# Three transformer blocks on one core: ends of the mixers, projections and feed-forwards issued as one stream of units

## What is computed

```python
def block1(h):                      # 528 tokens
    h = h + mixer_1(rmsnorm(h))     # 3 attention branches; below is how the mixer ends
        # merged = sum over 3 branches of sigmoid(g_b + bias) * (y_b @ w_br_b); then merged @ w_out
    z = rmsnorm(h) @ w_up           # 2 x 2816 columns
    gate, val = split(z)
    return h + (silu(conv3(gate) + b) * val) @ w_down
def block2(x):
    x = x + mixer_2(rmsnorm(x) @ w_in) @ w_out
    x = x + same_feed_forward_form(rmsnorm(x))
    return rmsnorm(x)
def block3(h, c):
    sh1, sc1, g1, sh2, sc2, g2 = split(silu(c) @ w_ada + b_ada)
    h = h + g1 * (mixer_3((rmsnorm(h) * (1 + sc1) + sh1) @ w_in) @ w_out)
    h = h + g2 * (square(relu((rmsnorm(h) * (1 + sc2) + sh2) @ w_ff1)) @ w_ff2)
    return rmsnorm(h)
# rmsnorm(a) = a * rsqrt(mean(a*a over the 1024 features) + 1e-6) * gain
```

## Time and profile before

| | us |
|---|---|
| median of 3 runs | 3058.05 |
| the profiled execution | 3077.81 |
| its span | 3075.5 |
| TensorE matmuls busy (mean granted clock 0.941) | 2847.3 (93%) |
| TensorE weight loads busy | 2335.3 (76%) |
| VectorE busy | 1517.5 (49%) |
| ScalarE busy | 1066.4 (35%) |
| GpSimd busy | 101.6 (3%) |
| DMA, mean | 78 GB/s |

### The profile page before, as it was taken

The page is one execution under the profiler, slowest core; times in us unless marked ns, Lnnn a source line. Parts: engine busy times, 40 slices in busy tenths (PEclk is TensorE's granted clock), DMA queues, the critical chain, the costliest instruction groups (busy, mean ns, idle before and its releaser), DMA issues. The chain is left out here.

```text
span 3075.5 us, 40714 instructions
## 1 busy us (share of the span) xinstructions
PE 2847.3 (93%) x16096; PEld 2335.3 (76%) x16096; DVE 1517.5 (49%) x2420; ACT 1066.4 (35%) x1882; POOL 101.6 (3%) x89
## 2 busy tenths in 40 slices
PE   7999999899999979979988999898899899899998
PEld 6778888889999857867745788675676568678786
DVE  3786643644444462164454666543663453433443
ACT  3365444432222341423333322233332332332222
POOL 0053210000000000000000000000000000000000
PEclk9999999999999997879878999999999999999999
DMA  3111111222222312210002455332121112222221
GB/s 122 61 49 53 51 63 56 70 74 91 89 89 88 119 56 79 68 34 2 1 1 103 165 190 186 108 103 69 62 76 55 35 62 96 76 82 95 83 95 69
DMA packets 70834, 240.13 MB, mean 78 GB/s; under 512 B 12084, under 2 KB 12981, under 8 KB 70302
## 3 DMA queue, kind: packets, MB, share of 16 engines
q1 hardware_dynamic: 63054, 210.19, 20.6%
q10 hardware_dynamic: 7632, 27.86, 2.6%
HBM read 235.37 MB, written 2.64 MB: 77 GB/s over the span
## 5 line engine op out<-in xcount | busy, mean ns | idle before, releaser
L473 PE MATMUL ps<-xh,wh 128*128 128x258 f32 (+1 forms) x2352 | 721.7, 348 | 59.6 <-DVE xl L640 37.2
L473 PE MATMUL ps<-xl,wh 128*128 128x258 f32 (+1 forms) x2352 | 707.7, 342 | 0.0
L473 PE MATMUL ps<-xh,wl 128*128 128x258 f32 (+1 forms) x2352 | 705.2, 341 | 0.0
L473 PEld LDWEIGHTS ps<-xh,wh 128*128 128x128 f32 x2352 | 409.0, 191 | 132.0 <-issue 62.8
L418 ACT ACTIVATE wh<-ring 128x1024 fp32r<-128x1024 f32 x224 | 238.0, 1063 | 776.1 <-PE ps L473 765.9
L473 PEld LDWEIGHTS ps<-xl,wh 128*128 128x128 f32 x2352 | 408.4, 191 | 55.6 <-issue 5.7
L473 PEld LDWEIGHTS ps<-xh,wl 128*128 128x128 f32 x2352 | 409.4, 191 | 50.9
L432 DVE TENSOR_TENSOR wl<-ring,wh 128x1024 fp32r<-128x1024 f32 x224 | 274.3, 1225 | 316.2 <-ACT wh L418 316.1
L447 DVE TENSOR_TENSOR wl<-ring,wh 128x1024 fp32r<-128x1024 f32 x150 | 187.2, 1248 | 434.5 <-ACT wh L441 434.1
L455 PE MATMUL ps<-xh,wh 128*128 128x512 f32 x728 | 324.3, 446 | 27.3 <-DVE wl L447 13.6
L455 PE MATMUL ps<-xl,wh 128*128 128x512 f32 x728 | 297.8, 409 | 0.0
(11 more groups left out here) (395 smaller groups left out, 3352.9 us busy)
## 6 DMA issues: line engine op xcount, KB each, us to landing
ring<-in_weights SPq DMA_DIRECT2D x374, 512.0 KB, 3.5
arena<-in_w_ada ACTq DMA_DIRECT2D x48, 512.0 KB, 4.9
arena<-in_cmp_w SPq DMA_DIRECT2D x2, 2048.0 KB
h<-in_x ACTq DMA_DIRECT2D x4, 528.0 KB, 6.4
arena<-strip_scratch SPq DMA_DIRECT2D x8, 264.0 KB, 3.8
out_features<-arena SPq DMA_DIRECT2D x8, 256.0 KB, 2.2
tail<-in_nsa_consts SPq DMA_DIRECT2D x1, 1320.0 KB, 6.1
con<-in_consts SPq DMA_DIRECT2D x1, 801.0 KB, 11.3
```

Source lines behind the costliest of these rows:

```text
L473: last = pe.matmul(out(e), w[:, k, :], x[:, k, o:o + m], start=(k == 0 and n == 0), stop=(k == chunks - 1 and n == 2))
```

## The change

The plain functions, their blocks and their hardware loops are gone. `Merged`, `add_product`, the feed-forwards, the last norm of the second block and the modulation become stages of the same `run` as the projections that follow (`mixing_end` and second block's projections; `mixing_end_2` and the whole third block). Four `run`s remain, at whose ends engines meet: the first block's attention; from `Merged` to the second block's projections; the second block's attention; and one from its output projection to the end.

- `Line` replaces `Tiles` and the loops over tiles: units with a number of chunks, a choice of PSUM banks, and waits on whoever drained a bank last (`claim`).
- `Inputs` replaces input chunk k as soon as the last unit of the stage before has read it (`chunk_used`, semaphore `left`) and its source is ready.
- For norms without shifts (first feed-forward, second block's projections, second feed-forward), `Inputs` takes only the gain, and 1/norm is multiplied into the matmul's result: in `Glu` by GpSimd, once into the gate ahead of the convolution and once into the silu output; in the second block's `Projected` by VectorE, which then writes the tile in place of ScalarE's copy.
- `Sums` adds the squares of tiles 0 to 6 up on GpSimd, and TensorE multiplies only two tiles by ones (that sum and tile 7) instead of eight.
- `SecondRoot` derives the third block's first norm from sums taken before the second block's last norm is applied; `Residual` applies that one later. `Normed` is the old normed input with shifts.
- Behind the gate of the first feed-forward, 512 columns are computed instead of 516: the value units and the down product, each a single matmul of 512 columns where there were two of 258.
- `Modulation` takes two sums every 1.75 units, over 42 units.
- `Convolved`, `Gated` and `Merged` keep their work and get done-semaphores for the stage that reads them.

The core of the diff (`Added` is `add_product`'s addition as a `Line`, `Squared` is `act_mul`, `Later` shifts a stage's times):

```diff
+class Line(Stage):
...
+    def __init__(self, core, n, at, cols, banks, inputs=None, chunks=NC):
+        self.core, self.n, self.at, self.cols, self.banks, self.inputs, self.chunks = core, n, at, cols, banks, inputs, chunks
+        self.first, self.d = core.taken, chunks / NC
...
+        self.left = core.take("input_used", chunks - 1)
+        core.chunk_used = [(self.left.sem, self.left.at(k + 1)) for k in range(chunks - 1)] + [(core.used, core.taken)] + core.chunk_used[chunks:]
...
+    def claim(self):
+        core, self.opened = self.core, []
+        for u in range(self.n):
+            held = [self.bank(u) + b for _, _, b in self.pattern(u)]
+            waits = []
+            for b in held:
+                if b in core.drained and core.drained[b] not in waits:
+                    waits.append(core.drained[b])
+            self.opened.append(waits)
+            for b in held:
+                core.drained[b] = self.drain(u)
...
-                yield self.at + u + k / NC
+            wh, wl = core.wh[:, s % 2], core.wl[:, s % 2]
+            for k in range(self.chunks):
+                yield self.at + (u * self.chunks + k) / NC
                 if k == 0:
-                    if self.free.at(u - 1) > 0:
-                        pe.wait_ge(self.free.sem, self.free.at(u - 1))
+                    for sem, value in self.opened[u]:
+                        pe.wait_ge(sem, value)
                     pe.wait_ge(core.split_done, s + 1)
-                if self.x and u == 0:
-                    self.x.ready(pe)(k)
-                last = core.chunk(pe, s, k, lambda e: self.place(u), self.T, k == 0, k == NC - 1)
-            last.then_inc(core.used, 1)
+                if u == 0 and self.inputs:
+                    pe.wait_ge(self.inputs.lo.sem, self.inputs.lo.at(k + 1))
+                for i, (w, x) in enumerate(((wh, core.xh), (wh, core.xl), (wl, core.xh))):
+                    for e, (o, m, _) in enumerate(self.pattern(u)):
+                        last = pe.matmul(self.place(u, e), w[:, k, :], x[:, k, o:o + m], start=(k == 0 and i == 0),
+                                         stop=(k == self.chunks - 1 and i == 2))
+                if k == self.chunks - 1:
...
+class Inputs(Stage):
...
+        self.hi, self.lo = core.take("input_hi", len(tiles)), core.take("input_lo", len(tiles))
+    def scalar(self, act):
+        for k, a in enumerate(self.tiles):
+            yield self.at + (k + 1) / NC + 0.02
+            if self.free[k]:
+                act.wait_ge(*self.free[k])
+            if self.ready:
+                self.ready(act, k)
+            act.activation(self.core.xh[:, k, 0:self.T], a, ACT.Copy, scale=self.gains[k] if self.gains else 1.0).then_inc(self.hi.sem, 1)
+    def vector(self, dve):
+        for k, a in enumerate(self.tiles):
+            yield self.at + (k + 1) / NC + 0.14
+            dve.wait_ge(self.hi.sem, self.hi.at(k + 1))
+            xh, xl = self.core.xh[:, k, 0:self.T].bitcast(F32), self.core.xl[:, k, 0:self.T]
+            if self.gains:
+                ins = dve.scalar_tensor_tensor(out=xl, in0=a, scalar=self.gains[k], in1=xh, op0=ALU.mult, op1=ALU.subtract)
+            else:
+                ins = dve.tensor_tensor(xl, a, xh, ALU.subtract)
+            ins.then_inc(self.lo.sem, 1)
...
+class Normed(Stage):
...
+                                     in1=self.core.xh[:, k, 0:SEQ].bitcast(F32), op0=ALU.add, op1=ALU.subtract).then_inc(self.lo.sem, 1)
+        for k in range(NC):
+            yield self.at + 0.28 * k
+            if k == 0:
+                dve.wait_ge(self.columns.sem, self.columns.at(1))
+                dve.wait_ge(self.root.sem, self.root.at(1))
+            if k >= 2:
+                part(k - 2)
+                dve.wait_ge(self.lo.sem, self.lo.at(k - 1))
...
+class Sums(Stage):
...
+    def scalar(self, act):
+        core = self.core
+        for k in range(NC):
+            yield self.at + (k + 1) * self.d + 0.25
+            self.ready(act, k)
+            if k >= 2:
+                act.wait_ge(self.added.sem, self.added.at(max(1, k - 2)))
+            act.activation(self.sq[:, k % 2], self.tiles[k], ACT.Square, scale=self.gains[k] if self.gains else 1.0).then_inc(
+                self.squared.sem, 1)
+        yield self.end() + 0.55
+        if self.first is None:
+            core.exp_ln(act)
+            act.wait_ge(self.summed.sem, self.summed.at(1))
+            r = self.r.rearrange("p (s n) -> p s n", s=len(halves(self.T)))
+            core.act.do(act, act.activation(r, self.total(), ACT.Ln, bias=core.c("eps6"), scale=1.0 / D))
+            act.activation(self.r, self.r, ACT.Exp, scale=-0.5).then_inc(self.root.sem, 1)
+    def pool(self, pool):
+        for k in range(1, NC - 1):
+            yield self.at + (k + 1) * self.d + 0.4
+            pool.wait_ge(self.squared.sem, self.squared.at(k + 1))
+            if k > 1:
+                pool.wait_ge(self.added.sem, self.added.at(k - 1))
+            pool.tensor_tensor(self.acc, self.sq[:, 0] if k == 1 else self.acc, self.sq[:, k % 2], ALU.add).then_inc(self.added.sem, 1)
+    def tensor(self, pe):
+        for n, a in enumerate((self.acc, self.sq[:, (NC - 1) % 2])):
+            yield self.end() + (-0.3, 0.4)[n]
+            if n == 0:
+                pe.wait_ge(self.added.sem, self.added.at(NC - 2))
+            else:
+                pe.wait_ge(self.squared.sem, self.squared.at(NC))
+            for e, (o, w) in enumerate(halves(self.T)):
+                last = pe.matmul(self.core.ps[:, self.bank + e, 0:w], self.core.c("ones"), a[:, o:o + w], start=(n == 0), stop=(n == 1))
+        last.then_inc(self.summed.sem, 1)
...
+class SecondRoot(Stage):
...
+    def vector(self, dve):
+        yield self.one.end() + 0.8
+        dve.wait_ge(self.one.root.sem, self.one.root.at(1))
+        self.core.vec.do(dve, dve.tensor_tensor(self.t, self.r, self.r, ALU.mult))
+        dve.wait_ge(self.two.summed.sem, self.two.summed.at(1))
+        dve.tensor_tensor(self.t, self.core.ps[:, self.two.bank, :], self.t, ALU.mult).then_inc(self.scaled.sem, 1)
+        yield self.one.end() + 1.3
+        dve.wait_ge(self.made.sem, self.made.at(1))
+        dve.tensor_tensor(self.both, self.t, self.r, ALU.mult).then_inc(self.root.sem, 1)
...
+class Glu(Line):
...
+        for p in range(FT):
+            t, j = self.at + 2 * p + 1, p % 2
+            yield t + 0.35
+            if p == 0:
+                pool.wait_ge(self.sums.root.sem, self.sums.root.at(1))
+            pool.wait_ge(self.gate_in.sem, self.gate_in.at(p + 1))
+            g = self.gate[:, j, SEQ + 4 - self.wide:]
+            pool.tensor_tensor(g, g, self.r_gate, ALU.mult).then_inc(self.gate_scaled.sem, 1)
+            yield t + 1.08
+            pool.wait_ge(self.silu.sem, self.silu.at(p + 1))
+            pool.tensor_tensor(self.mid[:, j, 2], self.mid[:, j, 2], self.r, ALU.mult).then_inc(self.scaled.sem, 1)
...
+def down(core, at, up, hidden, n, tiles, banks, scale=None, before=None):
+    stages = []
+    for g in range(0, n, NC):
+        m = min(NC, n - g)
+        last = before or up
+        ready = (lambda g: lambda eng, k: up.ready(eng, g + k))(g)
+        inputs = Inputs(core, [hidden[:, g + k] for k in range(m)], at - last.d, SEQ, ready=ready)
+        before = Added(core, at, WHOLE, banks, inputs, m, tiles, scale)
+        stages += [inputs, before]
+        at += NC * before.d
+    return stages, before, at
...
+class Projected(Line):
...
+    def vector_first(self, dve, u):
+        if not self.sums:
+            return
+        if u == 0:
+            dve.wait_ge(self.sums.root.sem, self.sums.root.at(1))
+        dve.wait_ge(self.core.used, self.first + u + 1)
+        dve.tensor_tensor(self.dst[:, u], self.place(u), self.sums.r, ALU.mult).then_inc(self.free.sem, 1)
...
+class Modulation(Stage):
...
+    def when(self, n):
+        return self.at + 1.3 + self.every * (n // 2)
...
                 for k in range(lo, hi):
+                    if t == 0:
+                        pe.wait_ge(self.inputs.lo.sem, self.inputs.lo.at(k + 1))
                     for i, (w, x) in enumerate(((wh, core.xh), (wh, core.xl), (wl, core.xh))):
                         for e, (o, c) in enumerate(halves(T)):
                             last = pe.matmul(core.ps[:, self.place(n) + e, 0:c], w[:, k, :], x[:, k, o:o + c],
                                              start=(k == lo and i == 0), stop=(k == hi - 1 and i == 2))
+                    if t == NC - 1 and k in (0, 2, 4, 5, 6):
+                        last.then_inc(self.left.sem, 1)
                 last.then_inc(self.branch.sem if b < 2 else core.used, 1)
...
+    inputs = Inputs(core, sources, -1.2, T)
+    merge = Merged(core, T, G, merged, m, inputs)
+    stages = [inputs, merge]
+    inputs = Inputs(core, merged, NC - 1, T, ready=merge.ready)
+    both = [[(0, T // 2, 0), (T // 2, T // 2, 1)]]
+    out = Added(core, NC, both, (0, 2, 6), inputs, NC, h)
+    stages += [inputs, out]
```

(28 more changed lines are left out.)

885 lines of the change are left out of this document (344 added, 541 removed).

## The result

The changed kernel takes 2957.07 us, the median of 4 runs (2953.28 to 2957.27), against 3060.19 (3052.46 to 3066.27, 4 runs) before: a ratio of 0.9661, 95% interval 0.9637 to 0.9686. The gain is 103 us where 125 were forecast. The profiled execution took 2957.27 us, its span is 2955.5 and its mean granted clock 0.956.

A forecast was written before the change was run, and what follows sets the result against it. The prediction took TensorE's own work plus its idle seams as the bound. Stage savings summed to 133.9 us, less 9 for stream stalls, net 125, so 3058 - 125 = 2933 us; range 2914 to 2967.

The forecast's parts named there:

- What bounds it: Whole kernel: the span is TensorE's own work plus idle seams; other engines count only where TensorE waits for them.
- The prices: TensorE: unit of 24 matmuls 5.55 us at 512 columns, 5.80 at 516; square matmul 0.87; restart 1.8 lost.
- What the stream costs: 9 us: Streamed seams: stalls behind `Merged`, both `Glu`s, into second block's projections and at ones matmuls sum to 9 us, bounds 0 and 20.
- I allow 0 to 12 us and take 0: Up stages: modulation sums falling into the GpSimd chain cost 0 to 12 us for all 24, taken as 0.
- at nothing or at twice 1.54 changes no term: Up stages: a GpSimd multiplication, priced at 1.54 us, could cost nothing or double without changing the sum.
- the cover of 4 us: Up stages: GpSimd operations stay hidden from TensorE up to about 4 us each; the 2933 us sum holds that long.
- The evictions: Second block's projections: 26 tiles leave PSUM by VectorE, 0.69 us each; one or two in each of two places count, 2 us.
- Rival (a): Second block's projections become VectorE's: all 26 evictions on the path, 18 us instead of 2, 2949 us; chance 0.12.
- The gain is the same number of units in either: Whole kernel: the gain summed against the profiled 3077.8 us applies equally to the median, 3058 - 125 = 2933 us.
- No idle over 2 us: Sign of being right: TensorE never idle over 2 us from 552 to second block's factors, nor from its w_out to last down tile.
- The 11 us between the second down product and the third block: Sign of being right: about 11 us between second down product and third block; the norm chain was summed to 11.3.
- rival (b): Seams: in-order ScalarE and VectorE queues wait crosswise, half the old idle stays at nine seams, plus clock; 2963 us, chance 0.11.

The follow-up runs named there:

- e9: Changed kernel with streaming alone undone: every input chunk waits for the last product of the stage before, splits moved to suit; 2984.38 us.
- e13: Changed kernel with six more products with the matrix of ones in each of the stream's six norms, results thrown away; 2989.02 us.
- e4: Changed kernel in which the input of the two up stages waits for 1/norm, with the sum of squares ahead of it; 2966.84 us.
- e12: The changed kernel run again, unedited; 2953.75 us.
- e11: Changed kernel with VectorE multiplying the gate from PSUM, modulation sums every 2 units after GpSimd's work, products of ones later in TensorE's queue; 2932.36 us.
- e1: Changed kernel with the 48 modulation sums taken over 32 of 1024 columns; 2951.07 us.
- e2: Changed kernel with full modulation sums every 2 units instead of 1.75, placed after GpSimd's second multiplication and before the next weight split; 2948.97 us.
- e5: Changed kernel with each of the 84 GpSimd multiplications of the up stages done twice; 3005.20 us.

## Why the prediction was right or wrong, point by point

- **What bounds it.** Right. It is TensorE's own work plus its seams, and the removals that shorten one or the other carry the gain: streaming about 30 us (e9), the products of ones 30 (e13), 1/norm out of the input 10.6 at two of its three seams (e4), and the columns 8 to 11 (from the paces). The rest, some 20 to 25 us, is the joined programs, the chain of two norms, `Merged` and the third norm, which no run took apart.
- **The prices** of `Merged`, the relu stage with the last down product, the tail and the two norm chains came out within 0.4 us. A matmul of 512 columns takes 0.233 us in the up stages, not 0.2313, which makes 1.8 us in the second up stage and 0.7 in the first.
- **"What the stream costs: 9 us".** This is the term that was mis-sized: the rows of the seams fall some 21 us short of the sum, 12 more than the 9 allowed, and that is the larger part of the 22 us. Five places make most of it. The first down product fell 6.9 short. 1.7 of it are three stalls at its start. VectorE's timeline there:

```profile
889.93 1.22 DVE L387 TENSOR_TENSOR wl<-ring,wh 128x1024 fp32r<-128x1024 f32 x1 [3.14 <-ACT wh L381]
891.07 3.00 DVE L685 TENSOR_TENSOR xl<-arena,xh 128x512 fp32r<-128x512 f32 x3
894.00 0.53 DVE L923 TENSOR_SCALAR arena<-arena,par 128x512 f32<-128x512 f32 x1
...
896.02 3.60 DVE L685 TENSOR_TENSOR xl<-arena,xh 128x512 fp32r<-128x512 f32 x4
```

  The first `xl` takes 1.79 us instead of 0.68 behind GpSimd's multiplication, and the last convolution, 2 us, stands ahead of five of the eight `xl`. At the end of the same product come 3.0 us for GpSimd's addition, where I had the products "on the path" only by their own length and never asked whether they would be ready, and the half clock behind that: from this product of ones to the next it took 8.3 us, and 6.7 in e12, where the clock stayed. e11, with the products later in the queue, has no wait for GpSimd there. Behind `Merged` I had 2 us late; it was 1.73, but with the clock behind it, 3.1 in all. The second down product fell 3.6 short, by waits for `xl` (0.6 and 0.7) and for GpSimd's addition (0.8) and by the pace (0.9). The first unit of the second block's projections holds the product of tile 7 and 1.4 us of waiting for it (1029.23), 2.5 short. In the third block's w_out 1.5 us are a wait for `xl` at 2533.90, 1.9 short.
- **"I allow 0 to 12 us and take 0" for the modulation sums.** Wrong: about 4 us (e1, e2). The prediction named the collision, and then took the better end of its bounds. The second up stage's other shortfall, like the 2.3 us of the first, is the product of tile 7 that falls into it (0.9, charged to w_out), its wait of 0.4 to 0.5, and the pace.
- **GpSimd "at nothing or at twice 1.54 changes no term".** Right without sums (1.1 us in the first up stage, e5), wrong with them (45.6). That the sum stays as long as the cover of 4 us holds fell with it: a GpSimd instruction underway makes a modulation sum 1.1 us later, and it is those that push the convolution.
- **The evictions.** 0.8 us instead of 2. Rival (a) said 18.
- **"The gain is the same number of units in either."** This held for the changed stages. But the spans differ by 120 us and the medians by 103, since 17 us of the profiled execution of before lay in unchanged code, so a gain has to be read by stages and not as a difference of spans.
- **The signs.** "No idle over 2 us" failed at one place, the 3.0 us at 1020.93, and the half clock stood at two seams where the prediction had none (598.10, and behind 1020.93). The 11 us between the second down product and the third block came out.
- **The range** held the time only because of rival (b): its upper end is (b) and a little for the modulation sums. The time lies 24 us above the forecast, to which 0.58 had been given, and 6 us below (b), to which 0.11 had. Of (b) came true that in-order queues stall at the seams and that the clock falls behind some stalls; half of the old idle at nine seams did not stay.

## What to carry to other kernels

When a seam is streamed, write out for each in-order queue what stands ahead of the first urgent step, and ask of every operand when its producer is ready: the stalls left here are steps at the wrong place (a product that waits for GpSimd, a sum ahead of a convolution), and moving them cost nothing. Cover that is counted for one helper engine holds only as long as nothing else is in the queue between; measure it by doubling the helper's work. Replacing the work on the bottleneck engine (six of eight products of ones) gave about as much as all of the streaming.
